# A two-layer hybrid decoder trunk: attention in six units a layer, each of two heads, instead of sixteen units of one head and one query block

## The reference

```
h    = RMSNorm(x) * norm_w                      # each layer
proj = h @ w_in                                 # 1024 -> 4160 columns, split among the groups
# group 1: RWKV-7 time mixing (a recurrence over time), group 2: gated conv of width 3,
# group 4: RetNet retention; each is multiplied by SiLU of its own gate columns
# group 3, four heads of 64:
#   logits = q @ k.T / 8 + T5 bias(q_pos - k_pos), causal
#   (256-key blocks, top 3 of them: at 512 positions every past block is chosen)
#   y = softmax(logits) @ v, times SiLU(gate)
x    = x + concat(y1, y2, y3, y4) @ w_out       # 1024 -> 1024
# after the second layer: RMSNorm(x) * final_norm_w
```

## Time and profile before

| | |
|---|---|
| median of 3 runs | 700.94 us (700.02 to 701.28) |
| the profiled execution's own time | 700.66 us |
| its span in the profile | 698.4 us |
| mean granted clock of PE | 0.991 |
| busy: PE, PEld, DVE, ACT, POOL | 667.7, 512.1, 393.5, 187.4, 413.6 us |

### The profile page before, as it was taken

How to read it: one execution, slowest core, us unless ns; L and a number is a source line. 1 busy time by engine, 2 the same in 40 slices (tenths; PEclk the granted TensorE clock), 3 DMA queues, 4 the chain that set the end, 5 groups by cost and what they waited for, 6 DMA issues and landing times.

```text
span 698.4 us, 12012 instructions
## 1 busy us (share of the span) xinstructions
PE 667.7 (96%) x4955; PEld 512.1 (73%) x4955; DVE 393.5 (56%) x607; ACT 187.4 (27%) x357; POOL 413.6 (59%) x334
## 2 busy tenths in 40 slices
PE   4999999999999999979999999999999999997995
PEld 4778778878776666758887687787877666665884
DVE  5868963721366357873363996454116734678343
ACT  4343111221332333311134310131123223423111
POOL 4698996607543434568829799661743524327960
PEclk9999999999999999999999999999999999999998
DMA  8856333273212121254533323234622121007503
GB/s 249 255 166 190 91 91 95 65 157 102 52 42 61 32 60 32 61 153 119 166 105 91 77 75 91 75 85 73 155 62 57 37 61 31 1 18 222 153 0 121
DMA packets 122615, 66.85 MB, mean 96 GB/s; under 512 B 31358, under 2 KB 115906, under 8 KB 122434
## 3 DMA queue, kind: packets, MB, share of 16 engines
q1 hardware_dynamic: 122562, 66.08, 34.8%
HBM read 55.85 MB, written 10.22 MB: 95 GB/s over the span
## 4 chain that ended last, share of the span: by engine, by line
PE 87%; DVE 8%; DMA 1%; ACT 1%; issue 1%; SPq 0%; DVEq 0%; ACTq 0%
PE bank L627 22%; PE bank L628 20%; PE bank L629 20%; PE bank L806 3%; PE bank L790 3%; PE bank L772 3%; DVE act_lo L1582 2%; PE bank L798 2%; PE bank L725 2%; DMA pages<-in_x_dram 1%; PE bank L831 1%; PE bank L778 1%; DVE pages L1314 1%; PE bank L739 1%; DVE pages L1313 1%
## 5 line engine op out<-in xcount | busy, mean ns | idle before, releaser
L552 POOL TENSOR_TENSOR w_hi<-w_raw,constants 128x512 fp32r<-128x512 f32 x164 | 186.1, 1155 | 260.9 <-PE bank L629 199.9
L627 PE MATMUL bank<-act_hi,w_hi 128*128 128x512 f32 x656 | 271.6, 414 | 11.3 <-DVE act_lo L1582 5.4
L628 PE MATMUL bank<-act_hi,w_lo 128*128 128x512 f32 x656 | 256.9, 392 | 0.0
L629 PE MATMUL bank<-act_lo,w_hi 128*128 128x512 f32 x656 | 256.8, 392 | 0.0
L559 POOL TENSOR_TENSOR w_lo<-w_raw,w_hi 128x512 fp32r<-128x512 f32 x164 | 230.2, 1424 | 0.0
L627 PEld LDWEIGHTS bank<-act_hi,w_hi 128*128 128x128 f32 x656 | 123.4, 188 | 60.6 <-issue 23.5
L629 PEld LDWEIGHTS bank<-act_lo,w_hi 128*128 128x128 f32 x656 | 123.4, 188 | 27.1
L628 PEld LDWEIGHTS bank<-act_hi,w_lo 128*128 128x128 f32 x656 | 123.8, 189 | 23.8 <-issue 1.9
L1086 ACT ACTIVATE pages<-bank 128x512 f32<-128x512 f32 x24 | 14.3, 598 | 129.2 <-PE bank L629 129.2
L1593 DVE TENSOR_TENSOR x_or_y<-x_or_y,bank 128x512 f32<-128x512 f32 x16 | 11.0, 688 | 48.0 <-PE bank L629 48.0
L1429 DVE SCALAR_TENSOR_TENSOR pages<-bank,bias 128x128 f32<-128x128 f32 (+3 forms) x32 | 15.6, 487 | 37.6 <-PE bank L806 37.4
(11 more groups left out here) (176 smaller groups left out, 771.4 us busy)
## 6 DMA issues: line engine op xcount, KB each, us to landing
w_raw<-in_w_in_dram SPq DMA_DIRECT2D x66, 512.0 KB, 4.2
w_raw<-in_w_out_dram SPq DMA_DIRECT2D x16, 512.0 KB, 4.1
x_scratch<-x_or_y SPq DMA_DIRECT2D x16, 256.0 KB, 4.5
x_or_y<-x_scratch SPq DMA_DIRECT2D x16, 256.0 KB, 3.7
pages<-in_x_dram SPq DMA_DIRECT2D x4, 512.0 KB, 8.7
out_dram<-pages SPq DMA_DIRECT2D x4, 512.0 KB, 3.9
bias_scratch<-pages SPq DMA_DIRECT2D x1, 1280.0 KB, 7.3
constants<-in_consts_dram SPq DMA_DIRECT2D x1, 1128.5 KB, 6.9
```

The source lines that it names most:

```text
L552: pool.tensor_tensor(w_hi[:, i % HI, k, :], raw, const("one").unsqueeze(2).to_broadcast([P, H, P]), ALU.mult).then_inc(s("w_high"), 1)
L627: mm(b[:, :], hi, act_hi[:, k, :], start=n == 0, stop=False)
L628: mm(b[:, :], lo, act_hi[:, k, :], start=False, stop=False)
L629: ins = mm(b[:, :], hi, act_lo[:, k, :], start=False, stop=n == KT - 1)
```

## The change

The 16 units become 6 a layer: for each pair of heads, one unit of query blocks 0 and 1, one of block 2, one of block 3. A unit does both heads. Per step the parts are now `attend_scores`, `attend_turn` (transposes), `attend_norm` (the second half of DVE's softmax, a step of its own) and `attend_values`. Unit u has its scores in `after[11 + 2u]`, its scaling in `mid[12 + 2u]`, its transposes in `mid[13 + 2u]`, its values in `after[13 + 2u]`; so the last attention step is in slot 23, where it was in 28. The matmuls are the same ones with the same shapes, but those of the two heads alternate in scores and values; the scores of the two heads go to banks 2 and 3, the transposes to the same two. DVE does one reciprocal for a head's two blocks in a unit of two blocks; its other operations and ACT's exps are the same in number and shape. ACT's copies out of PSUM take both blocks in one.

```diff
+PARTS = ((0, 1), (2,), (3,))
+UNITS = 2 * len(PARTS)
...
-    for g in range(18):
-        after[11 + g].append(("attend", g))
-        if g in (9, 17):
-            after[11 + g].append(("attend_out", g // 10))
+    for u in range(UNITS + 1):
+
+
+        if u > 0:
+            mid[11 + 2 * u].append(("attend_turn", u - 1))
+            after[11 + 2 * u].append(("attend_values", u - 1))
+            if u % 3 == 0:
+                after[11 + 2 * u].append(("attend_out", u // 3 - 1))
+        if u < UNITS:
+            after[11 + 2 * u].append(("attend_scores", u))
+            mid[12 + 2 * u].append(("attend_norm", u))
...
+                def attend_scores(u):
...
+                    banks = [begin(f"s{u}_{hh}", layer) for hh in range(2)]
+                    for qb, c0, w in unit_blocks(u):
+                        last = qb == PARTS[u % len(PARTS)][-1]
+                        for hh in range(2):
+                            hr = head_rows(hh)
+                            ins = mm(banks[hh][:, c0:c0 + w], MQ[hr, p, qb * P:(qb + 1) * P], MK[hr, p, 0:w], start=True, stop=True)
+                            if last:
+                                end(ins, f"s{u}_{hh}", layer)
...
+                def attend_turn(u):
+                    first, n = unit_first(u), len(unit_blocks(u))
+                    for hh in range(2):
+                        pe.wait_ge(*at("prob_norm", layer, first + (hh + 1) * n))
+                        b = begin(f"pt{u}_{hh}", layer)
+                        for _, c0, w in unit_blocks(u):
+                            for c in range(c0, c0 + w, P):
+                                ins = pe.transpose(b[:, c:c + P], PB[:, hh, c:c + P], ident)
+                        end(ins, f"pt{u}_{hh}", layer)
...
+                def attend_values(u):
...
+                    for hh in range(2):
+                        pe.wait_ge(*read(f"pt{u}_{hh}", layer))
+                    yb = begin(f"moba_y{p}", layer) if part == 0 else ps(f"moba_y{p}", layer)
+                    for qb, c0, w in unit_blocks(u):
                         for kb in range(qb + 1):
-                            ins = mm(yb[hr, qb * P:(qb + 1) * P], rows["mv"][:, kb, h * N:(h + 1) * N],
-                                     PT[:, (g - 1) % 2, kb * P:(kb + 1) * P], start=kb == 0, stop=kb == qb)
...
+                            for hh in range(2):
+                                h = 2 * p + hh
+                                ins = mm(yb[head_rows(hh), qb * P:(qb + 1) * P], rows["mv"][:, kb, h * N:(h + 1) * N],
+                                         PT[:, hh, c0 + kb * P:c0 + (kb + 1) * P], start=kb == 0, stop=kb == qb)
```

More of the change, by code:

```diff
@@ L86, with unit_blocks, unit_first @@
 N_CONST = _at
+PARTS = ((0, 1), (2,), (3,))
+UNITS = 2 * len(PARTS)
+def unit_blocks(u):
+    out, at = [], 0
+    for qb in PARTS[u % len(PARTS)]:
+        out.append((qb, at, (qb + 1) * P))
+        at += (qb + 1) * P
+    return out
+def unit_first(u):
+    return sum(2 * len(PARTS[v % len(PARTS)]) for v in range(u))
 def layer_steps():
@@ L212, in bank_jobs @@
             any6(f"rot_{step[1]}")
[L213 to L220, removed]
+        elif kind == "attend_scores":
+            layer += [(f"s{step[1]}_{hh}", 2 + hh, 1) for hh in range(2)]
+        elif kind == "attend_turn":
+            layer += [(f"pt{step[1]}_{hh}", 2 + hh, 1) for hh in range(2)]
+        elif kind == "attend_values":
+            if step[1] % len(PARTS) == 0:
+                layer.append((f"moba_y{step[1] // len(PARTS)}", 4, 1))
         elif kind == "chunk_b":
@@ L778, in rotate @@
                     end(mm(b[:, :], const("rot"), RRAW[:, int(job[-1]), :], start=True, stop=True), f"rot_{job}", layer)
[L780 to L788, removed]
-                        for kb in range(qb + 1):
-                            ins = mm(yb[hr, qb * P:(qb + 1) * P], rows["mv"][:, kb, h * N:(h + 1) * N],
-                                     PT[:, (g - 1) % 2, kb * P:(kb + 1) * P], start=kb == 0, stop=kb == qb)
[L792 to L806, removed]
@@ new lines, in attend_scores @@
+                def attend_scores(u):
+                    p = u // len(PARTS)
+                    if u == 0:
+                        for j in ("mq0", "mq1", "mk0", "mk1"):
+                            pe.wait_ge(*read(j, layer))
+                    banks = [begin(f"s{u}_{hh}", layer) for hh in range(2)]
[6 more added lines that the diff above has]
+                                end(ins, f"s{u}_{hh}", layer)
@@ new lines, in attend_values @@
+                def attend_values(u):
+                    p, part = divmod(u, len(PARTS))
+                    if u == 0:
+                        for q in range(2):
+                            pe.wait_ge(*read(f"rows_mv{q}", layer))
+                    for hh in range(2):
+                        pe.wait_ge(*read(f"pt{u}_{hh}", layer))
+                    yb = begin(f"moba_y{p}", layer) if part == 0 else ps(f"moba_y{p}", layer)
+                    for qb, c0, w in unit_blocks(u):
+                        for kb in range(qb + 1):
+                            for hh in range(2):
+                                h = 2 * p + hh
+                                ins = mm(yb[head_rows(hh), qb * P:(qb + 1) * P], rows["mv"][:, kb, h * N:(h + 1) * N],
+                                         PT[:, hh, c0 + kb * P:c0 + (kb + 1) * P], start=kb == 0, stop=kb == qb)
+                    if part == len(PARTS) - 1:
+                        end(ins, f"moba_y{p}", layer)
@@ new lines, in attend_norm @@
+                def attend_norm(u):
+                    e, n_q = unit_first(u), len(unit_blocks(u))
+                    for hh in range(2):
+                        e += n_q
+                        dve.wait_ge(*at("prob", layer, e))
+                        link(dve.reciprocal(row_scale[:, 2 * hh:2 * hh + n_q], row_sum[:, 2 * hh:2 * hh + n_q]))
+                        for j, (_, c0, w) in enumerate(unit_blocks(u)):
+                            pb, n = PB[:, hh, c0:c0 + w], 2 * hh + j
+                            ts(pb, pb, row_scale[:, n:n + 1], None, ALU.mult).then_inc(s("prob_norm"), 1)
```

64 lines of the change are left out of this document (33 added, 31 removed).

## The result

The changed kernel takes 668.86 us (median of 4 runs, 667.36 to 669.63), before 700.48 in the same session; the ratio is 0.9549, 95% interval 0.9524 to 0.9574. That is 3.4 us under the forecast of 672.3 and 0.14 under the low end of the range. The profiled execution took 668.65 us, its span is 666.7 (before 698.4).

A forecast was written before the change was run, and what follows sets the result against it. PE was taken as the bound; 30.8 us saved there, less 2.2 of waits, plus 0.1 at the ends, took 28.7 off 700.66, giving 672.0, or 672.3 for the median. The range was 669 to 680.

The forecast's parts named there:

- What bounds: Whole kernel: PE, busy 667.7 of 698.4 us, so work taken off PE comes off the time unless a wait replaces it.
- Pairing, 17.3 us: Attention values and scores on PE: alternating heads halve the matmul time, saving 8.7 on values and 8.6 on scores.
- third and fourth rival: Alternating sections: one record longer each, +5, 677 us, chance 0.04; or no pairing in new forms, 689 us, chance 0.04.
- Changes of shape, 13.5 us: Attention on PE: saved by fewer changes, 48 sections a layer becoming 18 and 18 places becoming 9.
- 18 places at 0.20: Changes from and to the projection after the change: 9 places a layer, 18 in both, 3.6 us.
- 0.15 of a section of transposes: Attention transposes on PE: a change of shape charged at 0.15 us for each section, besides 0.11 a transpose.
- Waits, 2.2 us: PE waits added in the attention, 1.1 a layer: 0.5 at unit 1's transposes, 0.3 in `attend_values(4)`; others about even.
- first rival: Transposes: PE waits more because DVE's scalings still meet POOL, +7, 679 us, chance 0.12.
- The ends, 0.1 us gained: Layer ends: in layer 1 the 4.2 us wait for POOL gives way to waiting for the splits, gain 0.1.
- The sum: Whole kernel: 30.8 saved on PE, less 2.2 waits, plus 0.1 at the ends, 28.7 us off.
- 59.2 for the sections of before: Attention on PE before: values, transposes and scores at 7.4 us a head, four heads, two layers.
- second rival: Whole kernel better than the sum: no waits, and 1 or 2 us less at each layer's end, 668 us, chance 0.07.

The follow-up runs named there:

- e9: Changed kernel, but each place does values and scores of one head, then those of the other: 686.7 us, ratio 0.9815.
- e4: Changed kernel plus four extra 128x128 transposes at 14 places of bare projection (slots 24 to 30): 673.62 us, one execution.
- e5: Changed kernel plus four extra records of 64-row matmuls at 14 places of bare projection (slots 24 to 30): 678.07 us, one execution.
- e7: Changed kernel with `ret_finish` moved to slots 14 and 16 and unit 4's transposes ahead of the `ln_mean` step: 666.19 us, ratio 0.9518.
- e8: Kernel before, with SP's load of the final norm three weight loads later: 699.93 us, ratio 1.0006.
- e6: Changed kernel with eight units a layer, one query block each, attention ending in slot 27: 684.6 us, ratio 0.9773.
- e12: Changed kernel with its six units, all attention starting four slots later and ending in slot 27: 681.08 us, ratio 0.9737.

## Why the prediction was nearly right, and where it failed

**What bounds.** PE, as said: 31.4 us less busy, 31.7 off the span.

**Pairing, 17.3 us: right.** The wide scores take 1.06 for four records and the values 0.80 and 1.02, as forecast; the values and scores of a layer take 10.80 us against 10.7. With the pairing undone they cost 17.0 more (`e9`, 15.0 of it measured, the rest by rates). The third and fourth rival fell by the same rows.

**Changes of shape, 13.5 us: too low, and this is the step that failed.** "Transposes ... 6 or 8 of them, 0.81 or 1.03", and 18 places at 0.20. The 0.15 of a section of transposes was read at a place between values and scores, where both neighbours have another shape, and then charged beside the projection too, where it isn't paid (`e4` against `e5`). Unit 3's transposes, which stand alone between two quarters in slot 19, in the changed kernel:

```profile
234.71 0.39 PE L653 MATMUL bank<-act_lo,w_hi 128*128 128x512 f32 x1
234.94 0.82 PE L826 MATMUL bank<-constants,pages 128*128 128x128 f32 x6
235.51 0.48 PE L651 MATMUL bank<-act_hi,w_hi 128*128 128x512 f32 x1
235.83 0.40 PE L652 MATMUL bank<-act_hi,w_lo 128*128 128x512 f32 x1
```

0.23 in, 0.57 for six, 0.32 out. The transposes of both layers take 8.5 us, of which 0.8 is waiting inside a section: 7.7 instead of 10.6, so 2.9 us mis-sized. The places cost 3.1 instead of 3.6, another 0.5. Together 3.4, as much as the miss in the median; the other terms, below, are smaller and partly cancel. The trace of before held a hint already; unit 1's single transpose stood with no values ahead of it, and its start is 0.23 from the projection's record, the distance within a projection, where values and scores have 0.32:

```profile
201.33 0.39 PE L629 MATMUL bank<-act_lo,w_hi 128*128 128x512 f32 x1
201.56 0.27 PE L798 MATMUL bank<-constants,pages 128*128 128x128 f32 x1
```

**Waits, 2.2 us: right.** By distances of starts they are 1.18 a layer, 2.4 in all: 0.69 at unit 1 (0.5 forecast), 0.33 at unit 4's values (0.3), the rest three times about 0.05. `e7` took 1.9 of them back. The first rival did not come: scaling 384 keys takes 0.42 us, as forecast from its new place behind POOL's work, against the 1.25 of the earlier trace rows:

```profile
L1486 DVE TENSOR_SCALAR pages<-pages,small 128x384 f32<-128x384 f32 x8 | 3.4, 420 | 0.3
```

**The ends, 0.1 us gained: wrong in sign, small.** 12.80 and 13.06 us against 12.54 and 12.68, 0.6 lost. That the loss of POOL's wait brings nothing was right, and `e8` shows it apart.

**The sum again.** The stretches gave 32.2 where the sum had 28.6. Of the 3.6 the transposes and places are 3.4; values and scores take off 0.2 and the waits 0.2. The sum forgot the waits ahead of L798 that the kernel before had the earlier trace rows, 0.5 by starts, but its transposes were too dear there too, 13.6 where the starts give 13.05; so its 59.2 for the sections of before agrees with the measured 59.16, and nothing comes on top. 0.6 stays open. With the ends at -0.7 against the forecast, the span is 3.0 better. The second rival has the right time for the wrong reason: the waits came, and the ends grew. The range was too narrow below, since it let only waits and ends go better and held every price of PE as certain.

## What to carry to other kernels

Work that fills half of TensorE's array is worth putting beside work for the other half. Alternating records is the sure form, but both halves in one section give most of it; work of another shape between them takes all of it away. Price a change of shape by the neighbours that the section will have, not by the section: records of the projection's own shape paid only 0.09 us on the way back to it. And ask what stands in the queues at the new place: six units four slots later lost 12 us of the 32 gained. In the rows of its profiled execution 6.8 us are the last unit's waits, most of them for one ACT copy behind another group's step, and 3.3 an end of a layer at which a load had waited for that unit.

## What the runs showed of the hardware that was not expected

Sixteen records of values in two halves of the array, eight and then eight, took 1.49 us where the rates give 1.77 to 1.88 in the program's order; the starts read as if the second half began some four records, two matmuls, ahead of its turn. A return to the projection costs 0.09 us even from its own shape, and nothing on the way in. After its wait of 2.24 us in `e6` PE's granted clock was 0.50 from 277 to 279, and two products together took 1.4 us longer than at full clock; in `e12` a wait as long had no such effect. A split on DVE took 1.6 us while POOL split weights and 0.6 while POOL was idle.
